# Rotating MLA's shared key beside the relative bias instead of ahead of the sliding-window heads

## What is computed

```python
a = rms_norm(h, attn_norm[l])
proj = a @ w_in[l]
c_q, c_kv, k_rope, q_s, k_s, v_s = jnp.split(proj, IN_SPLIT_POINTS, axis=-1)
# mla_attention (8 heads): one rotated key part, shared by all heads
k_rope = apply_rope(k_rope_raw, cos, sin)
s = (jnp.einsum('bqhd,bkhd->bhqk', qn, k_nope)
     + jnp.einsum('bqhr,bkr->bhqk', qr, k_rope)).astype(jnp.float32) * scale
# swa_sink_attention (16 query heads, 2 key heads): adds a relative bias, looked up by distance
s = jnp.einsum('bnqhgd,bnkhd->bnhgqk', q, k_band).astype(jnp.float32) * (SWA_HEAD_DIM ** -0.5)
s = s + bias
```

## Time and profile before

| | us |
|---|---|
| median of 3 runs | 2610.37 |
| lowest and highest | 2610.24, 2611.01 |
| the profiled execution | 2610.18 |
| its span, first to last instruction | 2608.4 |
| around the span | 1.8 |
| TensorE (matmul) busy | 2582.1, 99% |
| VectorE busy | 1658.3, 64% |
| ScalarE busy | 1377.9, 53% |

### The profile page before, as it was taken

How to read it: one execution, slowest core, us unless ns; L and a number is a source line. 1 busy time by engine, 2 the same in 40 slices (tenths; PEclk the granted TensorE clock), 3 DMA queues, 4 the chain that set the end, 5 groups by cost and what they waited for, 6 DMA issues and landing times.

```text
span 2608.4 us, 32895 instructions
## 1 busy us (share of the span) xinstructions
PE 2582.1 (99%) x13278; PEld 2180.8 (84%) x13278; DVE 1658.3 (64%) x2064; ACT 1377.9 (53%) x2013; POOL 0.2 (0%) x4
## 2 busy tenths in 40 slices
PE   9999999999999999999999999999999999999998
PEld 7877888888888888887888888888888888888887
DVE  7685556555665567568788866544566655655566
ACT  5664454444444446668878845544444444444444
POOL 0000000000000000000000000000000000000000
PEclk9999999999999999999999999999999999999999
DMA  6533565666556655555454436544565556655554
GB/s 225 164 132 138 192 214 194 194 191 189 191 189 192 194 194 171 185 179 175 137 180 145 131 129 247 165 161 131 192 198 191 192 194 194 193 188 190 192 190 144
DMA packets 235534, 468.78 MB, mean 180 GB/s; under 512 B 8219, under 2 KB 17654, under 8 KB 234102
## 3 DMA queue, kind: packets, MB, share of 16 engines
q1 hardware_dynamic: 234246, 465.11, 55.0%
q10 hardware_dynamic: 1136, 1.58, 0.2%
HBM read 460.36 MB, written 6.29 MB: 179 GB/s over the span
## 4 chain that ended last, share of the span: by engine, by line
PE 49%; DVE 1%; ACT 0%; issue 0%; DVEq 0%; ACTq 0%
PE ps L1178 10%; PE ps L1180 10%; PE ps L1179 10%; PE ps L1217 9%; PE ps L1216 5%; PE ps L1572 1%; PE ps L1585 1%; PE ps L1714 1%; PE ps L1689 1%; PE ps L1552 0%; PE ps L1235 0%; DVE AC L2967 0%; PE ps L1537 0%; PE ps L1611 0%; PE ps L1625 0%
## 5 line engine op out<-in xcount | busy, mean ns | idle before, releaser
L2485 DVE TENSOR_TENSOR WL<-Wt,WH 128x1024 fp32r<-128x1024 f32 (+1 forms) x861 | 1038.0, 1210 | 721.3 <-ACT WH L1769 668.3
L1769 ACT ACTIVATE WH<-Wt 128x1024 fp32r<-128x1024 f32 (+1 forms) x861 | 894.9, 1046 | 768.1 <-PE ps L1180 503.1
L1178 PE MATMUL ps<-WH,XT 128*128 128x512 f32 (+1 forms) x1184 | 471.9, 399 | 0.5 <-DVE XT L2849 0.3
L1178 PE MATMUL ps<-WH,HT 128*128 128x512 f32 (+2 forms) x1176 | 457.9, 389 | 3.3 <-DVE WL L2485 3.3
L1180 PE MATMUL ps<-WH,XT 128*128 128x512 f32 (+1 forms) x1184 | 459.8, 388 | 0.0
L1179 PE MATMUL ps<-WL,XT 128*128 128x512 f32 (+1 forms) x1184 | 459.0, 388 | 0.0
L1180 PE MATMUL ps<-WH,HT 128*128 128x512 f32 (+2 forms) x1176 | 452.1, 384 | 0.0
L1179 PE MATMUL ps<-WL,HT 128*128 128x512 f32 (+2 forms) x1176 | 451.5, 384 | 0.0
L1217 PE MATMUL ps<-XT,WH 128*128 128x512 f32 x960 | 336.5, 394 | 0.0
L1217 PE MATMUL ps<-HT,WH 128*128 128x512 f32 x960 | 336.5, 394 | 0.0
L1216 PE MATMUL ps<-HT,WL 128*128 128x256 f32 x960 | 267.0, 278 | 0.0
(11 more groups left out here) (390 smaller groups left out, 1979.2 us busy)
## 6 DMA issues: line engine op xcount, KB each, us to landing
Wt<-in_mlp_w SPq DMA_DIRECT2D x128, 1024.0 KB, 5.2
Wt<-in_w_up SPq DMA_DIRECT2D x64, 1024.0 KB, 5.5
Wt<-in_w_down SPq DMA_DIRECT2D x64, 1024.0 KB, 5.0
Wt<-in_w_in SPq DMA_DIRECT2D x53, 1024.0 KB, 5.1
Wt<-in_w_out SPq DMA_DIRECT2D x32, 1024.0 KB, 5.0
Wt<-in_xa_wk SPq DMA_DIRECT2D x16, 1024.0 KB, 5.1
Wt<-in_xa_wv SPq DMA_DIRECT2D x16, 1024.0 KB, 5.1
Wt<-in_xa_wq SPq DMA_DIRECT2D x16, 1024.0 KB, 5.1
```

Source lines behind the costliest of these rows:

```text
L1178: pe.matmul(o, xh, wh, start=start, stop=False)
L1769: act.activation(m.WH[:, i % NR, 0:2 * w], m.Wt[:, slot % NW, h * 2 * w:(h + 1) * 2 * w], ACT.Copy).then_inc(*up("wsplit.a", i))
L2485: dve.tensor_tensor(m.WL[:, i % NR, 0:2 * w], m.Wt[:, slot % NW, h * 2 * w:(h + 1) * 2 * w], m.WH[:, i % NR, 0:2 * w].bitcast(F32), SUB).t ...
```

## The change

The three steps of the shared key leave the head of `gen_swa` and become a generator of their own, `gen_krope`. It is put into the list of generators after the group of columns that holds `k_rope` has been written out (in the pump of i7 or after), and it yields until `angle_parts` has been issued. `gen_swa` starts with the window keys. `rope_products` for the queries' second and third part now waits for the sums of the part before instead of for the key; the scratch tile `RT` is shared.

```diff
         p.do("angle_parts")
+        p.now("angles")
         yield
...
+    def gen_krope():
+        while not p.had("angles"):
+            yield
+        p.do("rope_products", "k")
+        yield
+        p.do("rope_sums", "k")
+        yield
+        p.do("krope_turn", *p.banks(1))
+        yield
+
     def gen_swa():
         while not p.had("proj", 4) or not p.had("ln1", "scale"):
             yield
-        p.do("rope_products", "k")
-        yield
-        p.do("rope_sums", "k")
-        yield
-        p.do("krope_turn", *p.banks(1))
-        p.now("krope")
-        yield
         p.do("swa_keys", *p.banks(1))
...
         p.now("proj", ci)
+        if ci == 2:
+            p.bg.append(gen_krope())
...
-            on.wait_ge(*at("rope.v", "kt"))
+            on.wait_ge(*(at("rope.v", c - 1) if c else at("rope.v", "kt")))
```

## The result

The changed kernel takes **2616.11 us** (median of 18 runs, 2614.28 to 2618.24). The kernel before, on the same chip, takes 2610.65 (18 runs, 2609.87 to 2611.99). The ratio is 1.0018, 95% interval 1.0012 to 1.0025: slower, by 5.5 us, just about the 0.2% that I called no change. The predicted 2614.0 is 2.1 too low. The range, 2609.5 to 2616.8, holds the median.

What follows compares the result with a forecast made beforehand. TensorE bounds the kernel, busy 2582.1 of 2608.4 us. Terms 1.19 + 0.90 + 0.77 + 0.76 - 1.87 + (6.23 - 1.66) - 1.87 - 0.60 - 0.28 = +3.6 gave 2614.0 us; 8 in 10: 2609.5 to 2616.8.

Steps and rivals of the forecast that it cites:

- The front: Moved rotation: new wait of 1.79 at the key's turn, old 0.6 at the second `onehot_turn` gone; net loss 1.19 us.
- swa_keys and the first pair: Window keys: loss 0.90; first pair of head groups: hg 0's turn +0.77, hg 3's first scores +0.76, hg 1's turn -1.87.
- The large term: Second pair of head groups: VectorE late, waits 3.46 at hg 2's turn and 2.77 at its value; 6.23 against 1.66.
- Rival A: Second pair of head groups: VectorE not late, 3.46 + 2.77 fall away, 2607.7 us, or 2610.9 if half; chance 0.15.
- The end: After hg 2's value: last wait -1.87, fewer interruptions -0.60, small gaps -0.28; first MLA turn at 202.2.
- TensorE's waits up by about 3 us: Sign to look for in the new profile: TensorE's waits in all up by about 3 us.
- Rival B: TensorE's clock falls at the second pair's new waits: one slow half 2616.7, two 2619.4; chance 0.13 with VectorE's upper bound.

Runs made afterwards that it cites:

- shortened division: Changed kernel with VectorE dividing only 8 of the 128 columns in hg 3's division: 2614.18 us.
- rotation alone: Changed kernel with only the rotation moved; swa_keys and the heads keep their old pumps: 2612.50 us, ratio 1.0005 to the kernel before.
- distance four: Changed kernel with the second pair's chain 1 four pumps behind chain 0 and not one: 2613.95 us.
- distance three: Changed kernel with the second pair's chain 1 three pumps behind chain 0, as before the change, and not one: 2612.64 us, ratio 1.0005.
- filled idle time: Changed kernel with one redundant matmul of 512 columns ahead of the scores at 156.6 us: 2614.82 us, ratio 1.0016.
- three repairs: Changed kernel with the key's turn one pump later, chain 1 three pumps behind chain 0, and VectorE's copies for the window keys issued earlier: 2610.54 us, ratio 0.9997.

## Why the prediction came out as it did

**The front: right.** Wait 1.61, and the old 0.45 gone. The second `onehot_turn` starts 66.34 - 64.58 = 1.76 later; 0.46 of that was there from the start, since a first transfer (`GRA`) landed later, a wait of 1.4 and not 0.9. 1.30 for a predicted 1.19.

**swa_keys and the first pair: right.** Brackets 0.99, 0.83 and 0.75 for displacements of 1.15, 0.77 and 0.76. The old wait at hg 1's turn is gone.

**The large term: right, to a tenth.** From the last scores to hg 2's turn 186.37 - 164.99 = 21.38, for 17.97 + 3.46 = 21.43. From there to its value 6.41, for 6.4. (21.45 - 17.97 is 3.48 and not 3.46, a slip without weight.) That a sum of 21 us of VectorE's rows came out so close is luck in part, but the shortened division and the changed distance show that it is the mechanism. Rival A, that VectorE would not be late, is out.

**The end: too hopeful.** Predicted from hg 2's value to the first MLA turn were 202.2 - (188.68 + 1.75) = 11.77 (1.75 is the displacement before it: 1.19 + 0.90 + 0.77 + 0.76 - 1.87). Measured: 205.11 - 192.78 = 12.33. Of the 0.60 for fewer interruptions and the 0.28 of small gaps, 0.56 did not come. Up to the MLA turn 6.50 were lost: 0.46 at the start, 1.69 by the clock, so 4.35 by the queues for a predicted 3.6. The sign "TensorE's waits up by about 3 us" was off too: the brackets between 55 and 199 us sum to 9.96 for 5.17 before, 4.8 more. The prediction's own list of waits, 10.70 new against 6.25 old, already gave 4.45 more. The 4.35 put a run without a fall at 2614.5 or so, where the first group lies.

**The clock: the step that failed.** I tied a fall to the two longest new waits, gave it 0.13, and argued against it from the earlier trace rows: 3.7 us without a matmul, still at 1.00. In the traces the fall is at a wait of 0.75 that I had in the sum as +0.76 and nothing more. Both traced runs of the changed kernel are of the upper group and have it; the eleven upper runs have mean clocks of 0.996 to 0.998, five of the seven lower ones 0.999, and the lower-group trace with the key's turn one pump later has no fall there. So it is most likely in 11 of 18 runs, and so in the median. Rival B had the right kind of event and nearly the right price (2616.7 for one slow half; measured 1.69 and not 2.72 per fall, since some eight of the half's twelve matmuls ran slow and not all; this on top of the 4.2 between the lower groups of the two kernels), but another place and by far too small a chance. What made a bad witness: it is one sample of one idle stretch at the end of a program. In the changed kernel the wait of 3.2 at hg 2's turn was followed by 1.00 in the first trace and by 0.50 in the second, and the wait of 0.75 was followed by 0.50 in both of these and by 1.00 with the key's turn one pump later; a single trace cannot say that a wait is safe. The Trainium skill, "TensorE: Matmul & The Clock Gate", section "Why this matters for your kernels", warns of idle gaps between bursts of matmuls. The traces agree that the clock can fall behind a gap, but a fall behind 0.75 of idle time, with 1.00 behind 3.2, shows that the length of a single gap does not decide it here.

**The total.** 2614.0 is the time of the likeliest case as I saw it, and seven runs are within 0.9 of it. The median lies in the other group, and the range holds it only because it reached up past the price of one fall (2616.7).

## What to carry to other kernels

A step moved "beside" other work still sits in three in-order queues: price it by what stands ahead of it in the queue of the engine that feeds it, and ask which later chains move with it; here two thirds of the loss came from two head chains that closed up to one pump apart. When TensorE is near 100% busy, count stretches of small matmuls with waits between them as places where the clock may fall, and give that a chance even where no wait is long. Look at the single times for groups before trusting a trace: a trace shows one group.

## What the hardware showed that I had not expected

- The granted clock fell to 0.50 for about 3.4 us behind waits of 0.75 (changed kernel, both traces, and short division), 1.59 (rotation alone), 2.58 (distance four) and 3.2 (changed kernel, second trace, and turn one pump later). It stayed at 1.00 behind 3.22 and 2.56 (changed kernel, first trace), 3.07 (distance three) and 0.75 (turn one pump later). In two traces (filled idle time, three repairs) it fell for some 6.8 us, beginning within a wait of 3.1 to 3.2.
- A fall of 3.4 us cost 1.6 to 1.7 us where TensorE had no wait behind it, and nothing where it had one.
- One added matmul of 0.9 us made the kernel 1.3 us faster in the median, by taking away a wait of 0.75 and with it, in the trace, the fall.
- A kernel on one core can have two groups of times 1.7 us apart. In the changed kernel the upper one has the fall in its traces, and in the kernel before the upper group has the lower mean clock.
